# Half of the expert weight transfers issued from ScalarE: the odd places of a ring of 16, with the even ones left on SyncE

## What is computed

```python
def expert_block(args):
    xblk, e = args
    return (jax.nn.silu(xblk @ w_gate[e]) * (xblk @ w_up[e])) @ w_down[e]
```

## Time and profile before

| | us |
|---|---|
| median of 3 runs | 2768.81 |
| lowest and highest | 2767.47, 2770.95 |
| profiled execution, its own time | 2768.57 |
| its span in the trace | 2766.8 |
| PE busy in the span | 2488.3 (90%) |
| ACT busy in the span | 626.7 (23%) |
| mean DMA rate over the span | 218 GB/s |
| SP's queue of transfers | 528.65 MB, 50.7% of the 16 engines' span |
| expert weights (three tensors, 128 transfers of 1024 KB each) | 26.7, 27.2 and 28.0 us from issue to landing |

### The profile page before, as it was taken

How to read it: one execution, slowest core, us unless ns; L and a number is a source line. 1 busy time by engine, 2 the same in 40 slices (tenths; PEclk the granted TensorE clock), 3 DMA queues, 4 the chain that set the end, 5 groups by cost and what they waited for, 6 DMA issues and landing times.

```text
span 2766.8 us, 32912 instructions
## 1 busy us (share of the span) xinstructions
PE 2488.3 (90%) x12755; PEld 1550.3 (56%) x12755; DVE 921.3 (33%) x1708; ACT 626.7 (23%) x1172; POOL 349.3 (13%) x409
## 2 busy tenths in 40 slices
PE   5999899999999698989985999899999888989994
PEld 3769566788884443333332768567886443333331
DVE  3344566522224720000004534556332730000003
ACT  2321344622210110111112321446331000111110
POOL 1231000001111221000002430000011211000001
PEclk8999999999999789999998999999999889999997
DMA  9571000322217679999996560004333789999994
GB/s 285 195 245 46 6 1 13 86 58 69 58 43 223 252 288 419 421 421 417 420 421 241 188 216 23 6 1 87 92 103 129 267 328 419 420 420 405 420 421 165
DMA packets 238331, 604.39 MB, mean 218 GB/s; under 512 B 67328, under 2 KB 143504, under 8 KB 188640
## 3 DMA queue, kind: packets, MB, share of 16 engines
q1 hardware_dynamic: 210786, 528.65, 50.7%
q0 software_dynamic: 24512, 63.13, 6.4%
q10 hardware_dynamic: 2880, 10.49, 0.9%
HBM read 585.70 MB, written 38.16 MB: 225 GB/s over the span
## 4 chain that ended last, share of the span: by engine, by line
PE 69%; DMA 14%; DVE 7%; ACT 3%; SPq 3%; issue 2%; POOL 0%; DVEq 0%; ACTq 0%; POOLq 0%
PE slot L1067 19%; PE abank L672 18%; PE vbank L672 11%; DMA arena<-in_w_down_e 6%; DMA arena<-in_w_up_e 6%; PE slot L978 5%; DMA arena<-in_w_in 2%; SPq L2557 2%; PE vbank L854 2%; DVE nmx L1479 1%; PE slot L881 1%; PE abank L752 1%; PE vbank L801 1%; ACT arena L1970 1%; PE vbank L914 1%
## 5 line engine op out<-in xcount | busy, mean ns | idle before, releaser
L1067 PE MATMUL slot<-arena 128*64 128x512 f32 (+2 forms) x3264 | 825.2, 614 | 87.9 <-DMA arena<-in_w_up_e 59.8
L1067 PEld LDWEIGHTS slot<-arena 128*64 128x64 f32 (+2 forms) x3264 | 296.0, 146 | 564.2 <-issue 551.8
L672 PE MATMUL abank<-round,round 128*128 128x512 f32 (+1 forms) x1792 | 492.1, 356 | 11.7 <-DVE round L1544 8.3
L672 PEld LDWEIGHTS abank<-round,round 128*128 128x128 f32 x1792 | 319.4, 190 | 74.3 <-issue 19.9
L1786 DVE TENSOR_TENSOR arena<-slot,arena 128x512 f32<-128x512 f32 x76 | 52.6, 692 | 807.0 <-ACT arena L2090 516.2
L672 PE MATMUL abank<-hT_low,round 128*128 128x512 f32 (+1 forms) x896 | 319.2, 356 | 0.0
L672 PE MATMUL vbank<-round,round 128*128 128x512 f32 (+2 forms) x1312 | 307.8, 361 | 1.7 <-issue 1.7
L672 PEld LDWEIGHTS vbank<-round,round 128*128 128x128 f32 x1312 | 227.6, 190 | 37.2 <-issue 3.2
L672 PEld LDWEIGHTS abank<-hT_low,round 128*128 128x128 f32 x896 | 169.6, 189 | 23.5
L1570 DVE TENSOR_TENSOR arena<-vbank,arena 128x512 f32<-128x512 f32 x72 | 43.4, 603 | 307.0 <-PE vbank L672 307.0
L978 PE MATMUL slot<-arena 128*128 128x512 f32 x320 | 140.1, 600 | 3.4 <-POOL arena L2253 3.4
(11 more groups left out here) (282 smaller groups left out, 2742.7 us busy)
## 6 DMA issues: line engine op xcount, KB each, us to landing
arena<-in_w_gate_e SPq DMA_DIRECT2D x128, 1024.0 KB, 26.7
arena<-in_w_up_e SPq DMA_DIRECT2D x128, 1024.0 KB, 27.2
arena<-in_w_down_e SPq DMA_DIRECT2D x128, 1024.0 KB, 28.0
arena<-in_w_ada POOLq DMA_DIRECT2D x80, 512.0 KB, 4.9
arena<-in_w_in SPq DMA_DIRECT2D x48, 512.0 KB, 4.0
arena<-in_w_in SPq DMA_DIRECT2D x8, 2048.0 KB, 14.6
h_rows<-arena ACTq DMA_DIRECT2D x20, 512.0 KB, 6.4
arena<-y_rows SPq DMA_DIRECT2D x20, 512.0 KB, 8.2
```

The lines of the kernel that those rows point to most:

```text
L672: last = pe.matmul(to, x, y, start=(k == 0 and q == 0), stop=(k == len(terms) - 1 and q == 2))
L1067: last = pe.matmul(to[at, cols], x[:, at], w[:, at_w, :], start=first, stop=final)
```

## The change

A helper `unit_loader(queue, L)` holds the code that SP had for a unit (wait for the place, expert number, transfer), now for any queue. SP issues units 0 to 15 as before, and of the later ones those with even n. ACT issues those with odd n, not in a loop of its own but at two kinds of steps of its walk: after the sigmoid of a block's gate, all odd units whose places are free by then by the order of the program, and after the copy of a block's result in the same way. So a place that was last read by up is filled again only after the next result copy. At block 0 ACT also waits for `eord_ready`. Even n is an even place of the ring, odd n an odd place.

```diff
+        def unit_loader(queue, L):
...
+            def load_unit(n):
+                i, part, half, e = units[n]
+                if n >= RAW:
+                    queue.wait_ge(unit_used, mark["unit_used", L, n - RAW])
+                at = expert(i, e)
...
+                    queue.dma_start(raw[n % RAW], src.rearrange("(p j) f -> p j f", j=4)).then_inc(raw_in[n % RAW], 16)
...
@@ scalar
+                load_unit = unit_loader(act, L)
+                waiting = [n for n in range(RAW, len(units)) if n % 2]
+
+                def reload(used):
+
+                    while waiting and mark["unit_used", L, waiting[0] - RAW] <= used:
+                        load_unit(waiting.pop(0))
...
                         act.activation(am[i % 3], slot[0][:, n % 2 * FE:n % 2 * FE + FE], ACT.Sigmoid).then_inc(sgm_ready, 1)
+                        if i == 0:
+                            act.wait_ge(eord_ready, L + 1)
+                        reload(mark["part_done", L, i, "gate"])
...
                         act.copy(yb[i % 2], slot[1][:, :]).then_inc(y_ready, 1)
+                        reload(mark["part_done", L, i, "down"])
@@ sync
                 for n in range(RAW, len(units)):
-                    load_unit(n)
+                    if n % 2 == 0:
+                        load_unit(n)
```

More of the change, by code:

```diff
@@ L570, in grid_block, with expert @@
             return ap[0].rearrange("(r b j) d -> b r j d", r=ROWS, j=BCOL)[b]
+        def unit_loader(queue, L):
+            wgf = a["w_gate_e"].rearrange("l e d f -> (l e d) f")
+            wuf = a["w_up_e"].rearrange("l e d f -> (l e d) f")
+            wdf = a["w_down_e"].rearrange("l e f d -> (l e f) d")
+            ranked = {}
+            def expert(i, e):
+                name = order[i][1][e]
+                if isinstance(name, int):
+                    return name
+                if name not in ranked:
+                    ranked[name] = queue.value_load(eord[name[1]:name[1] + 1, 0:1], min_val=0, max_val=NE - 1)
+                return ranked[name]
+            def load_unit(n):
[3 more added lines that the diff above has]
+                at = expert(i, e)
+                if part == "down":
+                    src = wdf[bass.ds(at * FE + (L * NE * FE + half * 256), 256), :]
+                    queue.dma_start(raw[n % RAW].rearrange("p (j h) f -> p j (h f)", h=2),
+                                    src.rearrange("(p j) f -> p j f", j=2)).then_inc(raw_in[n % RAW], 16)
+                else:
+                    w = wgf if part == "gate" else wuf
+                    src = w[bass.ds(at * D + (L * NE * D + half * 512), 512), :]
+                    queue.dma_start(raw[n % RAW], src.rearrange("(p j) f -> p j f", j=4)).then_inc(raw_in[n % RAW], 16)
+            return load_unit
         @block.tensor
@@ L2536, in _ @@
                     broadcast(brow[:, NG:36], a["b_re"][L]).then_inc(rows8_in, 16)
[L2537 to L2562, removed]
+                load_unit = unit_loader(sp, L)
                 for n in range(4):
```

## The result

The changed kernel takes 2783.76 us (median of 5 runs, 2779.31 to 2789.14); the kernel before, timed beside it, 2767.47 us (2763.62 to 2770.95). The ratio is 1.0066, with a 95% interval of 1.0053 to 1.0078. The forecast was 2783 us, in a range of 2768 to 2797. The profiled execution has a span of 2782.3 us against 2766.8 us.

A forecast was written before the change was run, and what follows sets the result against it. The prediction took the DMA engines, busy from the first refill on, to bound the mixtures. It summed 2 x (4 + 3) = +14 us on 2768.57, 2782.6, so 2783 us; own range 2774 to 2793, wider range 2768 to 2797.

The forecast's parts named there:

- The bound: In the mixtures: the busy DMA engines and the last unit's landing set the end; faster issuing can't help.
- Term 1: Start of each layer: ACT issues odd units late, queues run dry; +4 us each, between 3.1 and 5.6.
- Term 2: End of each layer: odd units trail and land one behind the other, PE ends later; +3 us each.
- further dry places: Elsewhere in the mixtures, thinnest at 1280 to 1300: late odd units leave DMA engines dry, some 5 us, in the range only.
- What was taken at nothing: ACT's issues in each layer: 88 units and 17 rank loads, 40 us on a mostly idle engine, counted as no cost.
- much slower: Rival: ACT's issues held back as SP's, 2.0 us instead of 0.33, delaying copies and sigmoids; 2807 us, chance 0.11.
- No change: Rival: the gap at the start is filled and the end keeps its order; 2769 us, chance 0.14.
- faster: Rival: SP no longer blocks and two streams fill the DMA engines better in the mixtures; 2759 us, chance 0.06.
- DMA share under 1 at 1003 to 1014: Sign at the start of layer 0: this window would show a DMA share clearly under 1.
- Later landings from ACTq: Sign: weights from ACTq would land later than those of SPq.
- A longer wait before block 2's up: Sign: PE would wait longer before the up of block 2; no size given.
- PE's waits for weights up by 5 to 9 us: Sign: PE's waits for weights in a layer would grow by 5 to 9 us.

The follow-up runs named there:

- e5: Changed kernel, but SP issues all units below 32 and from 176 on, ACT the odd ones between: 2766.64 us, ratio 1.0000 to the kernel before.
- e2: Changed kernel, but SP issues all units below 32 of each layer, ACT odd ones from 33 on: 2772.97 us, ratio 1.0025 to the kernel before.
- e7: Changed kernel, but ACT refills only behind the sigmoid of each gate: 2806.26 us, ratio 1.0154 to the kernel before.
- e3: Changed kernel, but SP issues all units from 176 on: 2776.37 us, ratio 1.0035 to the kernel before.
- e4: Changed kernel, but SP issues all units on one queue, odd ones as late as ACT would have: 2788.79 us, ratio 1.0079 to the kernel before.
- e6: Changed kernel with ACT also refilling behind rows and middle copies, and SP issuing units below 32 and from 176: 2766.44 us, ratio 1.0006 to the kernel before.
- e8: Changed kernel with parity swapped, ACT issuing even units and SP odd ones: 2785.06 us, ratio 1.0067 to the kernel before.
- e1: Changed kernel, but ACT refills also behind its rows copy and middle copy: 2770.38 us, ratio 1.0015 to the kernel before.

## Why the prediction was right

**The bound.** It said that the DMA engines set the end of a mixture and that faster issuing can't help. SP's issues fell from 2.0 to 0.33 us, and with both ends left to SP the time is that of before (e5: 1.0000). The Trainium skill, DMA: Bandwidth & Descriptors, section Issuing engines are not separate DMA queues, says that transfers started from any engine run on the same 16 DMA engines, and that starting them from several only saves the time of the issue; e5 agrees with it.

**Term 1, the DMA engines' part, forecast 4 us a layer.** Mechanism and place were right: ACT issued units 21 to 27 from 1012.8 on (forecast 1013.5), and the windows of the start show 3.2 and 2.4 us lost. But the last weight packet is later by 5.9 and 6.2 us. The sum had left out that the engines run thin elsewhere. The prediction wrote that they are full from the start to the end, with 1280 to 1300 in layer 0 as the thinnest place (0.99); in layer 1 the place at 2530 to 2550 already stood at 0.91 in the kernel before, and there the change lost 4.0 us more, the largest piece of the 6.2 us. Why the change makes that place drier is not shown. In the timed runs, taking the lateness at the start away is worth 11 us for both layers (e2), against 8 forecast. In the profiled executions it brings the last packet forward by 3.8 and 3.4 us. The place of the pair moves with it, but not one way: in layer 1 it loses 3.4 us in place of 6.0, in layer 0 it is drier than in the change (0.90 over 1271 to 1311, against 0.99). The mixture of layer 0 is still as long in e2 as in the change (494.9 us), because this execution has the long tail there that the change's has in layer 1.

**Term 2, the end, forecast 3 us a layer.** The order of landings is as forecast: both queues share, then ACTq alone. The Trainium skill, DMA: Bandwidth & Descriptors, section Queues, rings and completion order, says that each DMA engine takes turns between the queues that have work; the trace agrees, with 47.1% and 46.9% of the engines in a full stretch. The size was right only as a mean: the tail grew by 0.1 us in layer 0 and by 4.8 us in layer 1. Some of the 4.8 us is the clock: the 48 matmuls that take 12.22 us from 2710.46 on take 10.52 us at the same place of e7, and the granted clock was 0.50 of full speed from 2712 to 2714. e3 gives 9 us for both layers in the timed runs, against 6 forecast. e4 adds what the prediction took only as a remark: in one queue, in order of issue, the late unit costs more at the end, 6.4 and 5.9 us.

**How much of the hit was luck.** The profiled execution of the change has some 12 us in the DMA engines' part and 5 us in the tails, 17 us in all; the forecast had 8 and 6, and 5 us for further dry places, which it put into its range and not into its sum. The start (5.6 us) and the tails came out below the terms, and the place of the pair in layer 1 made up for it. So the forecast and the median (2783 and 2783.76 us) agree better than the terms do, and that part is luck. Which of these pieces are there in a given execution varies, as the table shows.

**What was taken at nothing.** ACT's 88 issues a layer were taken at nothing, and the 72 that e5 and e6 leave on ACT cost nothing that can be measured: 0.34 to 0.38 us each in the median, at ratios of 1.0000 and 1.0006. The *much slower* rival needed issues of 2 us on ACT. It did not come, but the reason given against it was not good: the prediction took SP to be blocked at ten open units, and eight places for each queue to be safely below. Counting the units issued less the packets landed, SP's issues before took 0.33 us in the median with fewer than six open and 2.0 us with six or more; at most 9.4 were ever open. With the change at most 5.8 units were open in one queue, so it stayed just below. *No change* falls by the interval, *faster* by the plateaus, which stayed at 420 GB/s.

**The signs it named.** DMA share under 1 at 1003 to 1014: 0.72. Issues at 0.33 to 0.5 us: yes. Later landings from ACTq: yes (24 to 26 us from issue to landing, against 20 to 22 on SPq). The first mixture longer: yes, by 5.9 us. A longer wait before block 2's up: no, the wait there is 6.34 us against 6.78, with a new one of 3.56 us for a gate weight ahead of it. PE's waits for weights up by 5 to 9 us in a layer: too much. They are in layer 0:

```profile
PE slot L1098 <- DMA arena<-in_w_up_e: 28.4, 10, 7.8
PE slot L1098 <- DMA arena<-in_w_gate_e: 7.4, 5, 3.6
PE slot L1098 <- DMA arena<-in_w_down_e: 4.6, 5, 1.4
```

That is 40.4 us against 31.8 + 5.7 and 2.2 us for gate weights, 39.7 in all; in layer 1 it is 39.6 against 36.1. The lost time does not stand in the waits, because PE is not equally fast in both: for the same number of matmuls it was busy 448.2 us against 444.9 in the mixture of layer 0, and 449.1 against 441.8 in that of layer 1, where the granted clock was 0.96 against 0.98. A slower clock is a rival that no experiment tests by itself. The rows speak against it as the main cause: in the windows of the two starts and of the pair in layer 1 the granted clock is 1.00, before and after, and between them the last landing sets the end. What it does cost stands at the two ends of layer 1: the 1.7 us in the tail, and 0.9 us at the first products (clock 0.50 against 0.60 in their first 4 us, so the first refill goes out 6.1 us after the start of the mixture in place of 5.3).

## What to carry to other kernels

When the DMA engines are the bound, a late refill costs time where the queues have nothing else to do: put such a refill on the queue whose engine can wait for its place, not behind another engine's work. Here the late refills in the middle were free (e5), and those at the start and at the end of the stretch were paid for. Where half of the transfers must go to a second queue, leave the first and the last turn of the ring to the engine that only issues. To find such a cost, look at the DMA share in short windows, at both ends and wherever the consumer frees places slowly, and at how long after the last landing the consumer ends, not at the mean share, which moved from 1.01 to 1.00, nor at the sum of the waits.

## What the runs showed of the hardware that I had not expected

In the profiled execution of the change 7 issues went out with ten or more units open on both queues together, at most 10.8, and each took about 0.34 us; no queue had more than 5.8 of them. e5 shows both in one kernel: the 19 issues with six or more open on their own queue took 2.6 us in the median, the others 0.34 us.

And ACT started one rows copy in each layer of the changed kernel's profiled execution late (at 1028.20, 15.76 us of idle before it, though PE had turned the rows by 1019.8):

```profile
ACT arena L2120 <- remote: 15.8, 1, 15.8
```

The trace names no releaser of the program for it. That copy starts 8.4 us after PE is through with the turning, and by it the first result copy and the four up units behind it come later too. It stands just behind ACT's first burst of four issues, but the burst is not needed for it: e5's execution, which has none there, shows the same copy 3.1 us late. e6, e7 and e8, timed on the same chip as e5, show it as well (3.1, 5.4 and 8.1 us); e1, e2 and e3, timed on another, do not, though ACT issues there too. What it is stays open, and what it costs the change is not separated. It is not needed for a loss: e2 and e3 are slower than the kernel before (1.0025 and 1.0035) without it, and e5, with the short one, is not (1.0000).
